# Input norm and the first two weight units in 16 half-width steps, with zero products between the first transposes

## The reference, cut to what matters

```python
hp = layer_norm(x_prompt, ln_in_g, ln_in_b)
hs = layer_norm(x_sample, ln_in_g, ln_in_b)
# hybrid_layer, for both groups with the same weights:
z = h @ w_in                      # 1024 x 2816: q, k, v of two attentions, u and v of a gMLP
qa, ka, va, qb, kb, vb, uc, vc = jnp.split(z, splits, axis=-1)
o_a = moba_attention(...)         # softmax(q k^T / 8 - slope * dist) v, 6 heads of 64, causal
o_b = stick_breaking_attention(...)
o_c = chunk_spatial_gating(...)
h = layer_norm(DEEPNORM_ALPHA * h + mixed @ w_out, ln1_g, ln1_b)
f = jnp.square(jax.nn.relu(h @ w_ff1)) @ w_ff2
h = layer_norm(DEEPNORM_ALPHA * h + f, ln2_g, ln2_b)
```

## Time and profile before

| | |
|---|---|
| time, median of 3 (lowest, highest) | 721.65 us (721.18, 724.95) |
| profiled execution: time, span from first to last instruction | 721.94 us, 720.1 us |
| busy: TensorE, its weight loads | 679.5 us (94%), 655.7 us |
| busy: VectorE, GpSimd, ScalarE | 375.7, 356.5, 265.6 us |
| mean granted TensorE clock | 0.986 |

### The profile page before, as it was taken

One profiled execution on the slowest core, in us unless ns is written; L12 is line 12 of the kernel. 1 busy time (PEld: TensorE's weight loads), 2 busy tenths in 40 slices (PEclk: granted clock), 3 DMA queues, 4 the chain that ended last, 5 costly groups with the idle time before them and its releaser, 6 DMA issues.

```text
span 720.1 us, 14217 instructions
## 1 busy us (share of the span) xinstructions
PE 679.5 (94%) x5574; PEld 655.7 (91%) x5574; DVE 375.7 (52%) x691; ACT 265.6 (37%) x493; POOL 356.5 (50%) x452
## 2 busy tenths in 40 slices
PE   2999999999998699989999999999999999999993
PEld 1789999999997379989999999999999999999992
DVE  5556465576654445879742543623525436235247
ACT  5465666677656233643221212212112122121112
POOL 2973333444446205436954555545545555455417
PEclk9999999999999899999999999999999999999998
DMA  5244321222446933200332222222222222222303
GB/s 212 88 139 145 101 65 56 89 73 74 133 137 204 319 124 117 88 30 10 138 118 88 73 103 67 89 96 78 95 87 74 92 83 87 89 86 87 117 1 124
DMA packets 32961, 73.42 MB, mean 102 GB/s; under 512 B 3666, under 2 KB 18546, under 8 KB 32914
## 3 DMA queue, kind: packets, MB, share of 16 engines
q1 hardware_dynamic: 25778, 68.73, 28.2%
q10 hardware_dynamic: 6576, 3.38, 1.6%
q0 software_dynamic: 560, 0.66, 0.5%
HBM read 67.15 MB, written 5.60 MB: 101 GB/s over the span
## 4 chain that ended last, share of the span: by engine, by line
PE 85%; DVE 5%; DMA 2%; POOL 2%; issue 2%; SPq 2%; ACT 1%; DVEq 0%; POOLq 0%
PE acc L1510 74%; PE o_bank L1586 2%; DMA k_t<-cache_k_b 2%; POOL w_lo L582 1%; POOL res L662 1%; PE t_bank L1572 1%; PE acc L1572 1%; DMA xin<-x_prompt 1%; PE acc L1602 1%; SPq L481 1%; PE t_bank L1685 1%; SPq L511 1%; PE s_bank L1562 1%; DVE x_st L1038 1%; PE acc L1489 1%
## 5 line engine op out<-in xcount | busy, mean ns | idle before, releaser
L582 POOL TENSOR_TENSOR w_lo<-w_raw,w_hi 128x256 fp32r<-128x256 f32 x360 | 288.7, 832 | 292.7 <-ACT w_hi L692 292.6
L1510 PE MATMUL acc<-h_hi,w_hi 128*128 128x256 f32 (+1 forms) x864 | 258.7, 299 | 3.1 <-DVE h_lo L1053 1.7
L1510 PE MATMUL acc<-h_lo,w_hi 128*128 128x256 f32 (+1 forms) x864 | 250.9, 290 | 0.0
L1510 PE MATMUL acc<-h_hi,w_lo 128*128 128x256 f32 (+1 forms) x864 | 250.5, 290 | 0.0
L692 ACT ACTIVATE w_hi<-w_raw 128x1024 fp32r<-128x1024 f32 x90 | 95.2, 1059 | 246.9 <-PE acc L1510 224.2
L1510 PEld LDWEIGHTS acc<-h_hi,w_hi 128*128 128x128 f32 x864 | 164.6, 191 | 6.1 <-issue 4.3
L1510 PE MATMUL acc<-m_hi,w_lo 128*128 128x256 f32 (+1 forms) x576 | 166.4, 289 | 0.0
L1510 PE MATMUL acc<-m_lo,w_hi 128*128 128x256 f32 (+1 forms) x576 | 166.4, 289 | 0.0
L1510 PE MATMUL acc<-m_hi,w_hi 128*128 128x256 f32 (+1 forms) x576 | 166.1, 288 | 0.0
L1510 PEld LDWEIGHTS acc<-h_lo,w_hi 128*128 128x128 f32 x864 | 164.7, 191 | 0.4
L1510 PEld LDWEIGHTS acc<-h_hi,w_lo 128*128 128x128 f32 x864 | 164.0, 190 | 0.0
(11 more groups left out here) (239 smaller groups left out, 787.1 us busy)
## 6 DMA issues: line engine op xcount, KB each, us to landing
w_raw<-weights SPq DMA_DIRECT2D x94, 512.0 KB, 3.2
k_t<-cache_k_a SPq DMA_DIRECT2D x16, 192.0 KB, 3.2
k_t<-cache_k_b SPq DMA_DIRECT2D x16, 192.0 KB, 6.0
xin<-x_prompt SPq DMA_DIRECT2D x4, 512.0 KB, 5.6
y_prompt<-y_n SPq DMA_DIRECT2D x8, 256.0 KB, 2.0
v_pg<-cache_v_a SPq DMA_DIRECT2D x8, 192.0 KB, 4.3
v_pg<-cache_v_b SPq DMA_DIRECT2D x8, 192.0 KB, 6.5
k_t<-cache_v_b SPq DMA_DIRECT2D x8, 192.0 KB, 4.0
```

Source lines behind the costliest of these rows:

```text
L582: op = pool.tensor_tensor(w_lo[:, slot, part], w_raw[:, stage, part], w_hi[:, slot, part].bitcast(F32), ALU.subtract)
L1510: mm = pe.matmul(out, w[:, slot, cols(k)], x[:, ks[k], halves(hf)], start=(fresh and k == 0 and pas == 0), stop=last)
```

## The change

It rewrites the start and reorders what follows it on ScalarE.

- The 8 steps of 544 columns become 16 steps q: half 1 (288 columns) for k = 0 to 7, then half 0 (256 columns) for k = 0 to 7. Each uses one of four PSUM banks (s_bank0, s_bank1, t_bank, o_bank in turn) instead of two pairs. VectorE reads the even steps, ScalarE the odd ones; ScalarE rounds all of them, VectorE makes all low halves. GpSimd makes none.
- TensorE multiplies units 0 and 1 step by step as the steps come, into four banks of acc, one for each unit and half. Unit 2 follows. Transposes for step q + 4 or q + 8 stand between.
- Products of zeros (`spin`, the cleared qbd tile, plain fp32) stand ahead of the first transposes and between them: 4 of 512 columns, then 3, 3 and 4 of 256.
- VectorE takes half of the next tile's statistics ahead of a tile's factors; the second prompt tile is normalised in halves; the last prompt tile's statistics and all normalisations of it move in between the steps, and ScalarE writes all tiles.
- GpSimd rounds unit 0's weights itself; its low quarters are released one by one. hi_done so counts one less.
- dist_r, sid_r, id_r, below_r are made by ScalarE, behind the steps.
- After units 0 and 1 ScalarE stacks queries and keys, then splits unit 4 and 5; unit 6's rounding moves behind item 0's probabilities and the second part of the queries into item 1.

```diff
+        def x_step(q):
+            hf, k = 1 - q // KT, q % KT
+            bank = (s_bank[0], s_bank[1], t_bank, o_bank)[q % 4]
+            return hf, k, bank[:, 0:WIDE[hf]], q % 2 == 1
+        def first_bank(u, hf):
+            return acc[:, 2 * (u % 2) + hf if u < 2 else hf, 0:WIDE[hf]]
...
 # GpSimd
-            lo_part(0, 0, 0)
-            for k in range(0, KT, 2):
-                pool.wait_ge(hi_even, k // 2 + 1)
-                pool.tensor_tensor(h_lo[:, k, :], x_n[:, k, :], h_hi[:, k, :].bitcast(F32),
-                                   ALU.subtract).then_inc(h_even, 1)
-                if k == 0:
-                    lo_part(1, 1 % STAGE, 1)
+            pool.wait_ge(w_loaded[0], 16)
+            pool.tensor_copy(w_hi[:, 0, :], w_raw[:, 0, :]).then_inc(w0_hi, 1)
+            pool.wait_ge(w0_hi, 1)
+            for a in range(4):
+                part = slice(2 * P * a, 2 * P * (a + 1))
+                pool.tensor_tensor(w_lo[:, 0, part], w_raw[:, 0, part], w_hi[:, 0, part].bitcast(F32),
+                                   ALU.subtract).then_inc(w0_lo if a < 3 else lo_done, 1)
+            lo_part(1, 1, 1)
             lo_part(2, 2 % STAGE, 2)
-            pool.tensor_copy(dist_r[:, :], dist[:, :]).then_inc(bias_ready, 1)
...
             lo_part(3, 3 % STAGE, 3)
...
 # ScalarE
-                hi_part(u % RING, u % STAGE, u, 2 * (u - RING + 1) if u >= RING else None, 16 * (u // STAGE + 1))
+                hi_part(u % RING, u % STAGE, u, max(3, 2 * (u - RING + 1)), 16 * (u // STAGE + 1))
...
+            for o in range(2):
+                x_std_step(o)
+                x_normal(o, slice(0, D_MODEL))
+            x_std_step(2)
+            x_normal(2, slice(0, D_MODEL // 2))
+            x_normal(2, slice(D_MODEL // 2, D_MODEL))
+            x_std_step(3)
+            act.wait_ge(const_loaded, 32)
+            for q in range(2 * KT):
+                x_high(q)
+                if q == 1:
+                    x_normal(3, slice(0, D_MODEL))
+                if q == 3:
+                    x_std_step(4)
+                    hi_part(1, 1, 1, None, 16)
+                if q == 5:
+                    x_normal(4, slice(0, D_MODEL))
+                if q == 7:
+                    hi_part(2, 0, 2, None, 32)
+                if q == 11:
+                    hi_part(3, 1, 3, None, 32)
+            act.wait_ge(const2_loaded, 32)
+            act.activation(dist_r[:, :], dist[:, :], ACT.Copy).then_inc(bias_ready, 1)
+            for h in range(H):
+                act.activation(sid_r[:, h, :], c_("ident"), ACT.Copy, scale=SLOPES[h]).then_inc(bias_ready, 1)
...
-            for u in range(3):
-                read_half(u)
-                hi_unit(u + RING)
-                if u == 0:
-                    stack_q_hi(0, 0)
-                elif u == 1:
-                    stack_k_hi(0)
-                else:
-                    stack_q_hi(0, 1)
+            read_half(0)
+            read_half(1)
+            stack_q_hi(0, 0)
+            stack_k_hi(0)
+            hi_unit(RING)
+            read_half(2)
+            hi_unit(RING + 1)
...
-                    if i and s == 0:
+                    if n == 0:
+                        hi_unit(RING + 2)
+                    if n == 1 or i and s == 0:
                         stack_q_hi(i, 1)
...
 # VectorE
+            for o in range(3):
+                x_stats(o, 0)
                 if o:
                     x_scale(o - 1)
+                x_stats(o, 1)
+            x_stats(3, 0)
+            x_scale(2)
+            x_stats(3, 1)
             dve.wait_ge(const_loaded, 32)
+            x_value(0)
+            x_scale(3)
+            for q in range(2 * KT):
+                if q + 1 < 2 * KT:
+                    x_value(q + 1)
+                x_rest(q)
+                if q in (1, 2):
+                    x_stats(4, q - 1)
+                if q == 4:
+                    x_scale(4)
...
 # TensorE
+            def spin(count, width=SEQ):
+                zeros = qbd[0][:, :, :, :].rearrange("p b c q -> p (b c q)")
+                for _ in range(count):
+                    pe.matmul(acc[:, 0, 0:width], zeros[:, 0:P], zeros[:, 0:width], start=True, stop=True)
+            pe.wait_ge(zeroed, 2)
+            spin(4)
             pe.wait_ge(const_loaded, 32)
+            for o, t in enumerate((QT, 0, 1)):
+                pe.wait_ge(x_norm, o + 1)
+                for q in range(4):
+                    turn_x(q, t)
+                spin((3, 3, 4)[o], SEQ // 2)
...
+            for q in range(KT):
+                pe.wait_ge(x_lo, q + 1)
+                if q % 2 == 0:
+                    pe.wait_ge(*((w0_lo, q // 2 + 1) if q < 6 else (lo_done, 1)))
+                first_unit(0, q)
+                turn_next(q + 4)
+                if q == 4:
+                    pe.wait_ge(lo_done, 2)
+                if q >= 4:
+                    first_unit(1, q - 4)
+            for q in range(4, KT):
+                first_unit(1, q)
+                pe.wait_ge(x_lo, KT + q - 3)
+                turn_next(q + 8)
+            for q in range(KT, 2 * KT):
+                pe.wait_ge(x_lo, q + 1)
+                first_unit(0, q)
+                first_unit(1, q)
```

More of the change, by code:

```diff
@@ L715, in _ @@
-            act.wait_ge(const_loaded, 32)
[L716 to L721, removed]
-                act.activation(h_hi[:, k, :], x_n[:, k, :], ACT.Copy).then_inc(hi_odd, 1)
-                if k == 1:
-                    hi_unit(1)
@@ new lines, in x_value, with x_rest @@
+            def x_value(q):
+                hf, k, bank, other = x_step(q)
+                if not other:
+                    dve.wait_ge(xt_ready, q + 1)
+                    dve.tensor_scalar(x_n[:, k, halves(hf)], bank, lnp[:, 0, k:k + 1], lnp[:, 1, k:k + 1],
+                                      ALU.mult, ALU.add).then_inc(xn_dve, 1)
+            def x_rest(q):
+                hf, k, bank, other = x_step(q)
+                dve.wait_ge(x_hi, q + 1)
+                if other:
+                    dve.wait_ge(xn_act, q // 2 + 1)
+                else:
+                    dve.wait_ge(xn_dve, q // 2 + 1)
+                dve.tensor_tensor(h_lo[:, k, halves(hf)], x_n[:, k, halves(hf)],
+                                  h_hi[:, k, halves(hf)].bitcast(F32), ALU.subtract).then_inc(x_lo, 1)
@@ L1161, in _ @@
                                              ALU.subtract).then_inc(m_ready, 1)
-                if i and n < ITEMS and s == 0:
+                if n == 1 or i and n < ITEMS and s == 0:
                     stack_q_lo(i, 1)
@@ L1528, in in_unit, with first_unit, turn_next @@
                         slice(6 * (c % 4), 6 * (c % 4 + 1)))
-            for u in range(3):
-                for c in range(8):
-                    if u == 0 and c < 4:
-                        pe.wait_ge(h_even, c + 1)
-                        pe.wait_ge(h_odd, c + 1)
-                    in_unit(u, c)
-                    if u == 0 and c == 0:
-                        turn_x(6)
-                        turn_x(7)
+            def first_unit(u, q):
+                hf, k, _, _ = x_step(q)
+                product(w_hi, w_lo, u, cols, h_hi, h_lo, range(KT), first_bank(u, hf), hf, slice(3 * k, 3 * k + 3))
+            def turn_next(q):
+                if q == 4:
+                    pe.wait_ge(x_norm, 4)
+                if q == KT:
+                    pe.wait_ge(x_norm, 6)
+                for t in (QT, 0, 1) if q < KT else (2, 3):
+                    turn_x(q, t)
+            for q in range(KT):
[4 more added lines that the diff above has]
+                turn_next(q + 4)
+                if q == 4:
+                    pe.wait_ge(lo_done, 2)
[9 more added lines that the diff above has]
+                first_unit(1, q)
+            pe.wait_ge(lo_done, 3)
+            pe.wait_ge(acc_dve, 1)
+            for q in range(KT):
+                first_unit(2, q)
+            pe.wait_ge(acc_act, 1)
+            for q in range(KT, 2 * KT):
+                first_unit(2, q)
             pe.wait_ge(bias_ready, H + 3)
```

128 lines of the change are left out of this document (48 added, 80 removed).

## The result

The changed kernel takes **725.24 us** (median of 13 executions), the kernel before 722.44 beside it: ratio 1.0044, 95% interval 1.0028 to 1.006. I had forecast 716.7, in a range of 712.5 to 720.5. That is inside the 0.5% that I had said a measurement can tell, but the whole interval lies above 1: a small loss, where I had forecast a gain. (One disturbed execution of the changed kernel took 2230 us and one of the kernel before 843; neither bears on the ratio of the others.) The profiled one took 724.05 with a span of 722.2; before's span was 720.1.

What follows compares the result with a forecast made beforehand. TensorE, busy 94% of the span, was taken as the bound, with time only where it idles or runs slow. Unit 4's gain of 4.1 to 5.9 us, middle 5.0, off 721.65 gave 716.7 us, range 712.5 to 720.5.

Steps and rivals of the forecast that it cites:

- Transposes of the first four steps: Start, TensorE: the last of them at 12.0 us with the clock risen by 8.5; 16.0 if all zeros run low.
- the prices of 0.5 and 0.8: VectorE, low half of 288 columns: 0.8 us while GpSimd works, 0.5 when it rests.
- held for a whole quarter on top of its own 0.5: Shared-port rival, chance 0.1: low halves meeting a GpSimd quarter take 0.5 + 0.74 us on twelve steps; 718.7 us.
- The hole at 21.1: TensorE in the start: a hole at 17 to 22 us, ended by GpSimd's second low part.
- the low part of unit 1: GpSimd in the start: ready at 22.4 us (18.95 + 3.45), from where TensorE is full.
- The mark: TensorE: units 0 to 2 done, 46.19 us before, forecast 42.4, or 40.6 without the low stretch.
- low stretch: TensorE, some 3 us in 20 to 27 us: 3.5 us at half clock rate, 1.75 lost; other bound none.
- unit 4 starts: Behind the mark: ScalarE's read of unit 3 holds it until 52.3 us, 56.4 before; 50.5 with high clock; TensorE there at 50.8.
- the 5.0 I booked: Gain at unit 4: the middle between 4.1 us and 5.9 with the clock high throughout, taken off 721.65.
- the rest to shift as a block: Behind the first 56.44 us: TensorE dense, every load hanging on work done, so the early gain carries through.
- my rivals: Whole kernel: everything light 0.2, 713.6 us; shared port 0.1, 718.7; zeros in the way 0.1, 721.6; slower 0.05, 723.9.
- something behind 60 us does not shift: Last sign listed that would show the forecast wrong, beside zeros delaying transposes past 12.5 or second low part after 24.

Runs made afterwards that it cites:

- e5: The changed kernel unaltered, run again as the yardstick of its group: 725.24 us.
- e1: The kernel before with 14 tiny zero products (56 instructions) ahead of its first transpose: 728.84 us, ratio to before 1.0096.
- e3: The changed kernel with SyncE's 16 page-table reads taken four at a time behind the loads of units 3 to 6: 723.42 us, ratio to before 1.0018.
- e6: The changed kernel with 256 spare waits in TensorE's program from unit 3 on: 725.72 us.
- e4: The changed kernel without its 14 zero products: 719.08 us, ratio to before 0.9957.
- e2: The changed kernel with 128 spare waits in TensorE's program from unit 3 on: 719.46 us, ratio to before 0.996.
- e8: The changed kernel with page reads spread and without the 14 zero products: 716.96 us, ratio to before 0.9933.
- e7: The changed kernel with page reads spread and 128 spare waits that move the loop's body: 716.82 us, ratio to before 0.9935.

## Why the prediction was wrong

**The start: right, a little too dear.** Transposes of the first four steps at 11.50 to 12.1 (forecast 12.0), first product at 13.98 with the step of the high clock (14.3). VectorE's first low half and its last three:

```profile
13.05 0.88 DVE L1089 TENSOR_TENSOR h_lo<-x_n,h_hi 128x288 fp32r<-128x288 f32 x1
...
29.50 2.26 DVE L1089 TENSOR_TENSOR h_lo<-x_n,h_hi 128x256 fp32r<-128x256 f32 x3
```

The last ends at 31.76, forecast 31.5. The sixteen low halves took 9.7 us, 0.41 to 0.88 each and 0.61 in the mean, between the prices of 0.5 and 0.8, and none was held for a whole quarter on top of its own 0.5 (the longest is the 0.88 at 13.05). The hole at 21.1 was there, 1.22 us, but the last ScalarE normalisation ended it and not the low part of unit 1, which was ready at 21.35 (forecast 22.4). The mark came at 40.48: forecast 42.4 with a low stretch of 3.5 us, 40.6 without. The low stretch was there (granted 0.50 from 22 to 24 us; by the step from 21.1 to 24.2, some 3 us for my 3.5) and did cost, by my estimate 1.5 us (3 us at half rate) for my 1.75, since TensorE has no wait from 21.1 to the mark. What made the mark early is that this unbroken stretch began at 21.11 instead of 22.4 (1.3 us) and took 19.4 us instead of 19.95.

**Behind the mark: right in kind.** (The sum has a slip that changes nothing else: by its own rows TensorE itself would be there at 51.0, not 50.8.) ScalarE waits for w_raw of unit 6 (1.38 us, I said about 3) and unit 4 starts at 50.20, where I had 52.3, or 50.5 at the high clock. At this place the gain is 6 us, more than the 5.0 I booked.

**The step that failed** is one sentence: "Behind them TensorE is dense and every load hangs on work done, so I take the rest to shift as a block." Two things did not shift.

First, the load of unit 8 does not hang on work done alone, but on SyncE, which has 10 us of page reads and 3 us of key loads ahead of it. I had looked past a queue whose reads are no DMA and count as nobody's busy time. Price: 1.9 us in the profiled execution (1.1 in e5's), 1.7 to 1.9 between the kernels with and without the mend.

Second, "dense" hid that the MLP is a loop in hardware whose code is fetched again in each round if its place is bad. The zeros, costed as 14 products in an idle place, were also 56 instructions ahead of it. Price: 5.1 us in the loop. Also, all five profiles with the loop at 169 or 170 (after, e1, e3, e5, e6) have a wait of 0.8 to 1.1 us near 275 to 279 us for wo_lo, and none of the nine others does; that makes the 6 us. In the changed kernel an instruction packet moves at 268 to 270 us, between the issue of that weight load and its late landing (ScalarE waits for it until 271.73); that the one delays the other is argued only.

With both mended the kernel takes 716.8, against the forecast of 716.7. That it fits so well is partly luck: at unit 4 the start had won 1 us more than I booked, and not all of it came through. Among my rivals none named either loss, and "something behind 60 us does not shift" stood only in the last line, without a price or a chance. The 716.8 is also of another kernel than the one I forecast, and against its own group's before it is a gain of 4.7 us, not 5.0.

**The zeros** I had as a condition of the good start. They raised the clock and brought no gain that shows, to about 1.5 us (e4 against e2, e8 against e7, and the marks of ten profiles), and they brought all of the 5 us: without those 14 products the change is a gain of 0.43%, with them a loss of 0.44%.

## What to carry to other kernels

When a change adds or removes instructions ahead of a long hardware loop (here a body of 1598), count them, and look at the instruction queue by stretch: packets in every round, where there were none, point to the place of the body, and spare waits ahead of it, or fewer instructions, mended it here. "The rest shifts as a block" has to be shown queue by queue, the DMA-issuing one first: list what it does that is no transfer. And a cheap way to raise the clock is worth only what the engine is waited for at that time; read the level from the duration of a product, since the granted clock of a stretch can say 1.00 where the products take twice as long.

## What the runs showed of the hardware

A body of 1598 instructions ran without a fetch at either back edge or between them when it began at places 41, 113, 114, 135 and 215 of a block of 256, and was fetched anew (9 packets from one back edge to the next, 8 behind the second) from 169 and 170, at 2.5 to 3 us a back edge for TensorE (5.1 us for two in the changed kernel; in e1 its span's 6.7 less 1.0 that it is late at the entry, 5.7). The bad zone is under 80 places wide (135 and 215 are free). Why there is one is not shown. By my count the body touches 7 blocks from a place up to 194 and 8 beyond it, a zone of 62 places; but so counted the bad 169 touches 7 and the free 215 touches 8. That 8 blocks fail where 7 pass fits the thirteen kernels only if the true places lie 41 to 59 further on than I count them (something loaded ahead of the program), and no run measures that; that one block of the store is being filled ahead is a guess at the reason. No run changed the length of the body.

The Trainium skill, "Runtime: NRT & Kernel Launch", Instruction fetch mechanics, says that TensorE's instruction memory is 128 KiB, 2048 instructions, refilled in 16 KiB blocks ahead of use, and that a taken branch to a target outside the current window of 2 blocks has to fetch it first. The packets of 16 KB agree. The window does not: a body of 1598 instructions is over 6 blocks, and its back edge needed no fetch in the nine kernels with the places 41 to 135 and 215, so that more than 2 blocks were at hand; the measurement decides. Where the fetch is needed, the price is the one above.

SyncE took 10 us for 16 reads of the page table (46.2 to 56.2), 0.6 each, though each is one number.
